# Weight pieces ahead of the stage work in the first projection, first sum of squares on TensorE alone, and the final norm's scaling moved

## What is computed

```python
def rms_norm(x, g):
    xf = x.astype(jnp.float32)
    y = xf * lax.rsqrt(jnp.mean(xf * xf, axis=-1, keepdims=True) + EPS)
    return (y * g.astype(jnp.float32)).astype(x.dtype)

# in layer(l, ...), l = 0: the mixer's input
h = rms_norm(x, p['norm_mix'][l])
z = h @ p['w_in'][l]               # [B | C | x_conv | x_lru | gate], 2560 columns
yb = RG-LRU(dwconv4(x_lru)) * gelu(gate)
# in memory_kv: keys and values of the memory
m = rms_norm(mem, g_mem)
# behind the last layer
y_prompt = rms_norm(x, norm_final)
```

## Time and profile before

| | |
|---|---|
| median of 3 runs | 1032.88 us (1032.79 to 1035.61) |
| the profiled execution's own time | 1033.01 us |
| its span, first to last instruction | 1031.2 us |
| PE busy | 1014.5 us (98%) |
| DVE, ACT, POOL busy | 555.7, 385.5, 102.2 us |
| PE in the chain that ended last | 91% of the span |

### The profile page before, as it was taken

How to read it: one execution, slowest core, us unless ns; L and a number is a source line. 1 busy time by engine, 2 the same in 40 slices (tenths; PEclk the granted TensorE clock), 3 DMA queues, 4 the chain that set the end, 5 groups by cost and what they waited for, 6 DMA issues and landing times.

```text
span 1031.2 us, 25089 instructions
## 1 busy us (share of the span) xinstructions
PE 1014.5 (98%) x10837; PEld 810.9 (79%) x10837; DVE 555.7 (54%) x980; ACT 385.5 (37%) x580; POOL 102.2 (10%) x123
## 2 busy tenths in 40 slices
PE   8899999999999999999999999999999999999996
PEld 8899999799999999999999888445544654554454
DVE  6899765588666655677977455213310331231144
ACT  6786452365555444357645145100100010010003
POOL 4113120020000001101312112000000000000000
PEclk9999999999999999999999999999999999999999
DMA  9545769756555653454668968799999999999997
GB/s 342 177 158 193 260 269 383 317 176 204 169 197 167 243 200 124 139 199 137 228 218 354 387 266 336 285 426 373 398 372 395 352 400 395 384 374 369 396 376 310
DMA packets 37808, 295.20 MB, mean 286 GB/s; under 512 B 4464, under 2 KB 4720, under 8 KB 9040
## 3 DMA queue, kind: packets, MB, share of 16 engines
q1 hardware_dynamic: 35504, 284.54, 73.0%
q0 software_dynamic: 2208, 9.23, 2.8%
HBM read 287.14 MB, written 6.58 MB: 285 GB/s over the span
## 4 chain that ended last, share of the span: by engine, by line
PE 91%; DVE 3%; ACT 2%; issue 1%; POOL 0%; POOLq 0%; DVEq 0%; ACTq 0%
PE ps L2137 33%; PE ps L1686 16%; PE ps L1687 16%; PE ps L1688 16%; PE ps L1939 1%; PE ps L1973 1%; PE ps L1959 1%; PE ps L1913 1%; PE ps L2173 1%; PE ps L2149 1%; PE ps L1831 1%; DVE wlo L1063 1%; ACT whi L663 1%; PE ps L2083 0%; PE ps L1949 0%
## 5 line engine op out<-in xcount | busy, mean ns | idle before, releaser
L1063 DVE TENSOR_TENSOR wlo<-raw,whi 128x1024 fp32r<-128x1024 f32 (+1 forms) x178 | 235.8, 1342 | 80.0 <-ACT whi L663 79.8
L1686 PE MATMUL ps<-a_hi,whi 128*128 128x264 f32 x928 | 266.6, 287 | 4.2 <-DVE wlo L1063 2.8
L1687 PE MATMUL ps<-a_lo,whi 128*128 128x264 f32 x928 | 263.8, 284 | 0.0
L1688 PE MATMUL ps<-a_hi,wlo 128*128 128x264 f32 x928 | 263.7, 284 | 0.0
L663 ACT ACTIVATE whi<-raw 128x1024 fp32r<-128x1024 f32 (+1 forms) x178 | 190.5, 1083 | 134.1 <-PE ps L1688 125.8
L1686 PEld LDWEIGHTS ps<-a_hi,whi 128*128 128x128 f32 x928 | 175.6, 189 | 6.5 <-DVE wlo L1063 3.1
L1687 PEld LDWEIGHTS ps<-a_lo,whi 128*128 128x128 f32 x928 | 175.5, 189 | 0.3
L1688 PEld LDWEIGHTS ps<-a_hi,wlo 128*128 128x128 f32 x928 | 174.8, 188 | 0.0
L2137 PE MATMUL ps<-raw,xg 128*32 128x352 f32 x1536 | 116.6, 460 | 0.0
L2137 PE MATMUL ps<-wide,xg 128*32 128x352 f32 x1536 | 115.1, 459 | 0.0
L2137 PEld LDWEIGHTS ps<-wide,xg 128*32 128x32 f32 x1536 | 50.2, 110 | 63.4 <-issue 63.4
(11 more groups left out here) (320 smaller groups left out, 1558.1 us busy)
## 6 DMA issues: line engine op xcount, KB each, us to landing
raw<-dense_in_dram SPq DMA_DIRECT2D x58, 1024.0 KB, 5.0
raw<-moe_in_dram SPq DMA_DIRECT2D x36, 1408.0 KB, 9.6
wide<-moe_in_dram SPq DMA_DIRECT2D x36, 1408.0 KB, 10.4
raw<-gu_in_dram SPq DMA_DIRECT2D x22, 1024.0 KB, 4.8
raw<-moe_in_dram SPq DMA_DIRECT2D x12, 1536.0 KB, 8.8
wide<-moe_in_dram SPq DMA_DIRECT2D x12, 1536.0 KB, 9.4
raw<-cache_in_dram SPq DMA_DIRECT2D x12, 1024.0 KB, 8.4
wcache<-cache_in_dram SPq DMA_DIRECT2D x12, 1024.0 KB, 7.1
```

The costliest lines, as they stand in the source:

```text
L1063: dve.tensor_tensor(wlo[m % 4][:, 0:w], raw[:, k % RAWS, c:c + w], whi[m % 4][:, 0:w].bitcast(f32), ALU.subtract).then_inc(lo_done, 1)
L1686: pe.matmul(out, w_hi, m_hi_, start=first, stop=False)
L1687: pe.matmul(out, w_hi, m_lo_, start=False, stop=False)
L1688: return pe.matmul(out, w_lo, m_hi_, start=False, stop=last)
```

## The change

It has five parts. In layer 0's first projection ACT and DVE take the second piece of a step ahead of the body: ACT's order becomes `hi`, `hi`, `body`, DVE's `lo`, evacuation, `lo`, `extra` (`weights_first`, for l = 0 alone). The first sum of squares runs over all eight tiles on PE, and POOL's additions for it are gone. At the end ACT multiplies tiles 0 to 3 by the final gain ahead of the root, DVE multiplies all four pairs by the reciprocal in four instructions, and PE takes the squared tiles in the order 4, 5, 6, 0, 7.

```diff
--- before.py
+++ after.py
@@ -327,7 +327,7 @@
         SQUARED = ["mix0", "mem", "co0", "lo0", "xattn0", "ffn0", "mix1", "co1", "lo1", "xattn1", "ffn1", "fin"]
         NORMS = [name for name in SQUARED if name != "ffn1"]
         order = {name: i for i, name in enumerate(NORMS)}
-        FOLDED = ["mix0", "mem", "co0", "lo0", "xattn0", "ffn0", "mix1", "co1", "lo1", "xattn1", "ffn1"]
+        FOLDED = ["mem", "co0", "lo0", "xattn0", "ffn0", "mix1", "co1", "lo1", "xattn1", "ffn1"]
 
         def y_part(buf, e, q):
 
@@ -546,7 +546,6 @@
             pool.wait_ge(consts, 3)
             pool.affine_select(out=ident[:], in_=ident[:], compare_op=ALU.not_equal, fill=1.0, base=0,
                                pattern=[[-1, 128]], channel_multiplier=1).then_inc(consts, 1)
-            fold("mix0", sq_x, 2)
             for l in range(DEPTH):
                 IN, V, KX, MIX, Q, O = places(l)
                 if l:
@@ -662,13 +661,15 @@
                 m = 2 * k + s
                 act.activation(whi[m % 4][:, 0:w], raw[:, k % RAWS, c:c + w], ACT.Copy).then_inc(hi_done, 1)
 
-            def step(off, k, body=None, split=True):
+            def step(off, k, body=None, split=True, weights_first=False):
 
                 if split:
                     hi(off, k + 2, 0)
+                if split and weights_first:
+                    hi(off, k + 2, 1)
                 if body:
                     body()
-                if split:
+                if split and not weights_first:
                     hi(off, k + 2, 1)
 
             def load_table(function, c=0):
@@ -814,7 +815,7 @@
                 for j, body in ((1, lru_conv_base), (6, short_conv_base)):
                     do[j] = lambda parts=(do.get(j), body): [fn() for fn in parts if fn]
                 for j in range(10):
-                    step(0, IN + j, do.get(j), split=l or j)
+                    step(0, IN + j, do.get(j), split=l or j, weights_first=l == 0)
 
                 def valued(j, body=None):
 
@@ -1041,10 +1042,14 @@
             for k in range(4, KT):
                 act.wait_ge(scat_add, rounds * 32 + (k + 1))
                 square(sq_f[:, k], x[:, k])
+            def gained(ks):
+                for k in ks:
+                    c = PK["g_fin"] + k
+                    act.activation(hf[:, k], x[:, k], ACT.Copy, scale=pk[:, 0, c:c + 1]).then_inc(fin_g, 1)
+
+            gained(range(4))
             root("fin", 1.0 / D)
-            for k in range(4, KT):
-                c = PK["g_fin"] + k
-                act.activation(hf[:, k], x[:, k], ACT.Copy, scale=pk[:, 0, c:c + 1]).then_inc(fin_g, 1)
+            gained(range(4, KT))
 
 
         @block.vector
@@ -1067,7 +1072,7 @@
                 b = bank_of(k)
                 return ps[:, b:b + 2, 0:w]
 
-            def step(off, k, read, extra=None, first=None, split=True, late=False):
+            def step(off, k, read, extra=None, first=None, split=True, late=False, weights_first=False):
 
 
                 if first:
@@ -1076,12 +1081,14 @@
                     lo(off, k + 2, 0)
                 dve.wait_ge(pe_done, off * 2 + (2 * k + 2))
                 read().then_inc(evac, 1)
+                if split and weights_first:
+                    lo(off, k + 2, 1)
                 if extra:
                     dve.wait_ge(evac, off + (k + 1))
                     extra()
                 if late:
                     lo(off, k + 2, 0)
-                if split:
+                if split and not weights_first:
                     lo(off, k + 2, 1)
 
             def root_reciprocal(name, w=T):
@@ -1268,7 +1275,7 @@
 
                 for j in range(10):
                     step(0, IN + j, scaled_in(j), (lambda: [fn() for fn in extras[j]]) if j in extras else None,
-                         split=l or j)
+                         split=l or j, weights_first=l == 0)
 
                 lo(0, V + 2, 0)
                 recurrence()
@@ -1671,11 +1678,8 @@
                     y_out(1)
                 scattered(r * 4 + 3, True)
             root_reciprocal("fin")
-            for k in range(4):
-                dve.scalar_tensor_tensor(out=hf[:, k], in0=x[:, k], scalar=col(0, "g_fin", k), in1=rstd[:],
-                                         op0=ALU.mult, op1=ALU.mult).then_inc(n_h, 1)
-            for k in (4, 6):
-                dve.wait_ge(fin_g, k - 2)
+            for k in (0, 2, 4, 6):
+                dve.wait_ge(fin_g, k + 2)
                 dve.tensor_tensor(hf[:, k:k + 2], hf[:, k:k + 2], over_pair(rstd), ALU.mult).then_inc(n_h, 2)
 
 
@@ -1764,11 +1768,10 @@
 
             def first_sum():
 
-                pe.wait_ge(n_fold, 1)
-                pe.matmul(ps[:, 4, 0:T], ones[:], sq_x[:, 0], start=True, stop=False)
-                pe.wait_ge(n_sq, sq_of("mix0", 4))
-                for i in (6, 7):
-                    last = pe.matmul(ps[:, 4, 0:T], ones[:], sq_x[:, i], start=False, stop=i == KT - 1)
+                for i in range(KT):
+                    if i % 2 == 0:
+                        pe.wait_ge(n_sq, sq_of("mix0", i // 2 + 1))
+                    last = pe.matmul(ps[:, 4, 0:T], ones[:], sq_x[:, i], start=i == 0, stop=i == KT - 1)
                 last.then_inc(n_ss, 1)
 
             def folded_sum(name, src, w=T):
@@ -2187,7 +2190,7 @@
                     gather_rows(it)
                 scatter(r * 4 + 3, 3)
             pe.wait_ge(n_rt, order["fin"])
-            for k in (4, 0, 5, 6, 7):
+            for k in (4, 5, 6, 0, 7):
                 if k:
                     pe.wait_ge(n_sq, sq_of("fin", k - 1))
                 else:
```

## The result

| | before | after |
|---|---|---|
| median of 4 runs | 1032.97 us (1032.79 to 1035.61) | 1045.86 us (1044.55 to 1046.71) |
| ratio, 95% interval | | 1.0119 [1.0101, 1.0138] |
| the profiled execution's own time | 1033.01 us | 1045.40 us |
| its span | 1031.2 us | 1043.7 us |
| mean granted clock of PE | 0.997 | 0.994 |

The kernel became 1.2% slower. The forecast was slower at 1039.9 us, with a range up to 1042.5; the time lies 3.4 us above that range. So the sign was right, and the size was not: +12.9 us by the medians (12.3 by the ratio) instead of +6.9.

The account below looks back on a forecast made before the run. PE was taken to bound the kernel nearly throughout. From 1033.0 us: -4.65 + 7.8 (three new waits) + 2.2 + 0.5 + 0.6 + 1.65 - 1.1 = +7.0, 1040.0, stated as 1039.9 us; range 1035.2 to 1042.5.

Parts of the forecast that it names:

- The second pieces ahead of the bodies: Chunk 3's second half: PE's 3.0 us wait and the 1.65 us of slow clock behind it go, -4.65 us.
- First gates: Middle of chunk 5: PE waits 1.8 us for the memory's root, whose chain now starts at the end of chunk 4.
- gates(2): Behind chunk 5: PE waits 3.6 us for the first sigmoids, as ACT's copy before them waits for chunk 5's end.
- Chunk 13: Its first piece comes 2.4 us too late, as the decays stand behind a copy awaiting chunk 7's end; bounds 0 to 3.5.
- Chunk 4: PE waits 0.5 us for chunk 2's evacuation, late behind the longer first sum; between 0 and 0.8.
- First sum: Start of the kernel: PE does eight sum matmuls instead of three, five more at 0.445 us, uncovered, +2.2 us.
- POOL's early transfers: First loads: lru_w's four transfers, issued from about 3 us, take time on full DMA engines, +0.6 us, between 0 and 1.0.
- The clock: Behind PE's new waits the granted clock drops once, +1.65 us; bounds none and two drops (3.3).
- The long wait goes and nothing takes its place: Rival: chunk 3's wait goes with no new waits at gates or chunk 13; -2.45 us, 1030.5 us; chance 0.06.
- Only the two waits at the gates: Rival: chunk 13 does not wait and the clock stays up; 1035.9 us, down to 1034.8; chance 0.15.
- More of everything: Rival: the clock falls twice and every early transfer delays chunk 0; 1042 to 1043.5 us; chance 0.1.
- The skill's drain: Rival: each ACT table switch pauses ACT 1.38 us more, as the Trainium skill says; 1048 us; chance 0.01.

Follow-up runs that it names:

- Experiment 12: The changed kernel with the old order in step 4 alone, all other steps in the new order; 1042.96 us, ratio 1.0098 to the kernel before.
- Experiment 4: The changed kernel with the old order in step 5 alone, all other steps in the new order; 1039.17 us, ratio 1.0057 to the kernel before.
- experiment 11: The changed kernel with the old order in step 7 alone, all other steps in the new order; 1042.91 us, ratio 1.0099 to the kernel before.
- experiments 8: The kernel before with the new order in step 1 alone and the new end; old sum and late transfers stay; 1030.18 us, ratio 0.997.
- 9: The kernel before with the new order in steps 1 to 3 and the new end; 1030.25 us, ratio 0.997.
- 2: The changed kernel with the old order of pieces in all steps; long first sum, early transfers and new end remain; 1036.38 us, ratio 1.0037.
- 10: The kernel before with all eight squared tiles summed on PE; old order, old end, lru_w transfers held back; 1033.46 us, ratio 1.0003.
- Experiment 1: The changed kernel with the clearing of lru_w and its four transfers held back behind the last squares of x; 1042.83 us, ratio 1.0086.
- experiment 7: The changed kernel with small matmuls on constants filling PE's waits, 14 before gates(2) and 10 before chunk 13; 1043.47 us, ratio 1.0086.
- experiment 6: The kernel before with the new end alone; 1032.20 us, ratio 0.9989.
- experiments 3: The changed kernel with the new order in step 1 alone, all other steps in the old order; 1034.31 us, ratio 1.001.
- 5: The kernel before with lru_w's clearing and four transfers issued ahead of POOL's additions of squares; old order and old sum; 1034.83 us, ratio 1.001.

## Why the prediction was right and wrong

**The second pieces ahead of the bodies: right, -4.65.** PE goes into chunk 3's second half without idle time, at full clock, and no work of DVE or ACT stepped into its place.

**First gates, 1.8: right.** ACT's copy waited for the end of chunk 4, and the root came 0.15 us before PE went on. Experiment 12 takes this one wait away by one step's order.

**gates(2), 3.6: right (3.5).** Experiment 4 takes it away by step 5's order.

**Chunk 13, 2.4: right (2.6).** The chain was forecast as 0.26 + 1.07 + 5.68 + 24.8 us behind the end of chunk 7. In the trace chunk 7 ends at 72.78 and chunk 13 starts at 104.70, 31.9 us later. The remark that what is taken ahead inside the chain is of the same size held as well, and experiment 11 shows the other side of it: with that copy back in its old place the chain gains only 0.8.

**Chunk 4, 0.5: right in size (0.6), wrong in its reason.** The prediction put this wait down to the longer first sum. But PE's time for chunk 4 and DVE's chain to it both start at the end of that sum, so its length cancels: experiments 8 and 9 have the old, short sum and wait 1.1 us there, and 2 and 10 have the long sum in the old order and wait nowhere behind chunk 3. The wait comes from the order, which takes away the wait at chunk 3 that had covered it.

**First sum, 2.2: right in after.** Experiment 10 shows that it is not a fixed price: in the kernel before it is 0.3 us by the ratio (interval -0.8 to 1.4), since there the wait and the clock behind it absorb it.

**POOL's early transfers: this step failed in size.** It took 0.6 us with a bound of 1.0, the share of the four transfers in the time of all DMA engines. That counts the bytes that stand ahead of the weights, and takes it that all others go on at the old pace. They did not: 0.26 MB more cost 0.71 MB of the rest in 9 us, and the first sum started 2.1 us later. Experiment 1 gives 1.7 of it back. The bound was wrong in kind: here the transfers' own time, 0.96 us of all engines, was no upper bound for what they did to a full queue. Why they cost more than their share stays open.

**The clock: this step failed in number.** The forecast took one drop of 1.65, with none and two as bounds. The size is right, 1.7 and 1.5. But both long waits were followed by one, and experiment 7 shows that PE's standing still brings them and that keeping it at work without changing the waits takes both away. "One drop" had been chosen as the middle of the bounds, not read from the rows: the one wait of this kind in before, 2.84 us, was followed by a drop, and two waits of like length were forecast. By that row two was the likelier number. The drop in the routing stage was not in the sum at all; it is 1.5 of the 12.5 us of the profiled execution. Its cause stays open. It came in four of the six profiles that have the new order in all steps or all but one (after, 1, 4, 7, not 11 and 12) and in none of the other eight, so the runs do not clear the change of it. Executions of before lose to the clock at times too: one took 1037.03 us at a mean clock of 0.993, another 1031.16 at 0.998, and where in the kernel is not on record. How much of the drop in this stage is in the median isn't known.

**The end, -1.1: right**, here and alone in experiment 6.

**The rivals.** "The long wait goes and nothing takes its place" fell with the first row of PE's waits. It is nearly true of step 1 alone, where only small waits, of at most 1.1 us, take its place (experiments 3 and 8). "Only the two waits at the gates" fell with chunk 13. "More of everything", two drops and the full price of the transfers, was given 1042 to 1043.5 and a chance of 0.1: it is what happened, and even it was short by the part of the transfers beyond 1.0 us and by the third drop. "The skill's drain" is out: in after each table load takes 1.28 us and the next instruction starts within 0.02 us of its end, and the wait at gates(2), with one load in its chain, was 3.5 and not 1.38 more. On this point the Trainium skill (ScalarE: Activation LUTs, "What ACT_TABLE_LOAD costs") and the trace differ, and the trace decides.

## What to carry to other kernels

When the order of two instructions on an engine is turned to cure one wait, look at every step of the loop: the copy for a buffer that frees at the end of a chunk carries that release over to all work behind it. Turn it only in the step whose wait it cures; here one step gave 1.8 us of gain in the profile (3.1 by the ratio together with the new end), and all steps together cost 8.5 against the old order (after against experiment 2). Count a forecast wait of PE that is as long as one which had a clock drop behind it with the drop, and treat loads that saturate the DMA engines as a place where any added transfer may cost more than its own time.

## What the runs showed of the hardware

**The clock after a wait.** PE's waits of this stage in all 14 profiles, by the idle time in the brackets, with what the granted clock did behind them:

| wait of PE, us | where | followed by a drop |
|---|---|---|
| 3.3 | gates(2): after, 1, 11, 12 | 4 of 4 |
| 2.8 | chunk 3: before, 6 | 2 of 2 |
| 2.4 | chunk 13: after, 1, 12, not 4 | 3 of 4 |
| 2.2 | chunk 3: 2, 5, 10 | 0 of 3 |
| 1.6 to 1.7 | first gates: after, 1, 4, 7, 11; chunk 13: 11 | 0 of 6 |
| 1.1 | chunk 4: 8, 9 | 0 of 2 |

At 2.4 us the same wait came with a drop and without one, so its length alone does not decide. Each drop cost 1.5 to 1.7 us. A wait that was 0.6 us shorter, without the drop behind it, was thus worth some 2.2 in experiment 10.

**A drop without a long wait.** In the routing stage the clock fell in 4 of 14 profiles (after, 1, 4, 7). Each time this began 2.6 to 3.1 us behind a wait of 0.7 us, and the same wait stands in the other ten profiles with no drop. All four have the new order in all steps or all but one, and so have two of the ten. What tells these apart stays open.

**The start of the kernel.** With late transfers of `lru_w` the first sum started between 20.56 and 20.97 us in all 6 profiles. With early ones it started between 22.56 and 24.12 in all 8, and in 5 of these 8 the clock fell once between 13.8 and 17.8 us, with chunk 0 and 1 waiting for their data; with late transfers it never did there.
